# Norms that add pairs of squares on GpSimd before TensorE sums them over the features

## The reference

```python
def _normalize(x):
    xf = x.astype(jnp.float32)
    mu = jnp.mean(xf, axis=-1, keepdims=True)
    var = jnp.mean(jnp.square(xf - mu), axis=-1, keepdims=True)
    return (xf - mu) * lax.rsqrt(var + LN_EPS)
...
def rms_norm(x, g, eps=NORM_EPS):
    xf = x.astype(jnp.float32)
    y = xf * lax.rsqrt(jnp.mean(xf * xf, axis=-1, keepdims=True) + eps)
    return (y * g.astype(jnp.float32)).astype(x.dtype)
```

## Time and profile before

| | before |
|---|---|
| median of 3 runs | 4008.68 us (4008.21 to 4012.08) |
| the profiled execution | 4003.51 us, its span 4001.8 us |
| TensorE busy | 3569.2 us, 89% of the span, 27600 records |
| VectorE busy | 2124.3 us, 53% |
| ScalarE busy | 1295.8 us, 32% |
| GpSimd busy | 148.9 us, 4% |
| mean granted clock of TensorE | 0.905 |

### The profile page before, as it was taken

One profiled execution on the slowest core, in us unless ns is written; L12 is line 12 of the kernel. 1 busy time (PEld: TensorE's weight loads), 2 busy tenths in 40 slices (PEclk: granted clock), 3 DMA queues, 4 the chain that ended last, 5 costly groups with the idle time before them and its releaser, 6 DMA issues. The chain is left out here.

```text
span 4001.8 us, 64978 instructions
## 1 busy us (share of the span) xinstructions
PE 3569.2 (89%) x27600; PEld 3286.5 (82%) x27600; DVE 2124.3 (53%) x3151; ACT 1295.8 (32%) x1795; POOL 148.9 (4%) x148
## 2 busy tenths in 40 slices
PE   7679999999995889999997599999699999769799
PEld 5469999989973868999885489998499998458599
DVE  4527885557714425767345437673657543253254
ACT  1314444444412113444212134442434442211143
POOL 0001111100000100000000000000000000011000
PEclk9769999989997879999996699999799999878699
DMA  8407885447721005767531047674057443200142
GB/s 360 181 32 273 309 310 206 186 172 270 276 102 42 3 1 198 303 231 304 204 122 59 5 174 300 236 301 175 3 219 303 169 178 131 84 1 2 63 173 91
DMA packets 74190, 675.50 MB, mean 169 GB/s; under 512 B 8416, under 2 KB 12544, under 8 KB 52096
## 3 DMA queue, kind: packets, MB, share of 16 engines
q1 hardware_dynamic: 29824, 500.52, 32.2%
q10 hardware_dynamic: 41472, 151.01, 9.9%
q0 software_dynamic: 2688, 20.97, 1.6%
HBM read 668.25 MB, written 4.23 MB: 168 GB/s over the span
## 5 line engine op out<-in xcount | busy, mean ns | idle before, releaser
L1020 DVE TENSOR_TENSOR w_split<-ring,w_split 128x1024 fp32r<-128x1024 f32 x705 | 874.7, 1243 | 611.2 <-ACT w_split L915 608.9
L842 PE MATMUL banks<-u_split,w_split 128*128 128x256 f32 x3840 | 1092.8, 285 | 7.8 <-DVE w_split L1020 6.2
L915 ACT ACTIVATE w_split<-ring 128x1024 fp32r<-128x1024 f32 x705 | 742.9, 1057 | 1077.4 <-PE banks L844 861.0
L843 PE MATMUL banks<-u_split,w_split 128*128 128x256 f32 x3840 | 1090.6, 284 | 0.0
L844 PE MATMUL banks<-u_split,w_split 128*128 128x256 f32 x3840 | 1090.3, 284 | 0.0
L842 PEld LDWEIGHTS banks<-u_split,w_split 128*128 128x128 f32 x3840 | 742.1, 193 | 11.3 <-DVE w_split L1020 8.2
L427 PE MATMUL banks<-bufs,ring 128*128 128x256 f32 (+2 forms) x2880 | 659.7, 392 | 101.5 <-PEq L2710 24.0
L843 PEld LDWEIGHTS banks<-u_split,w_split 128*128 128x128 f32 x3840 | 741.7, 193 | 0.9
L844 PEld LDWEIGHTS banks<-u_split,w_split 128*128 128x128 f32 x3840 | 741.3, 193 | 0.0
L427 PEld LDWEIGHTS banks<-bufs,ring 128*128 128x128 f32 (+2 forms) x2880 | 553.3, 193 | 208.9 <-issue 85.5
L842 PE MATMUL banks<-h_split,w_split 128*128 128x256 f32 x1920 | 543.6, 283 | 2.9 <-DVE w_split L1020 2.9
(11 more groups left out here) (354 smaller groups left out, 3050.6 us busy)
## 6 DMA issues: line engine op xcount, KB each, us to landing
ring<-stream SPq DMA_DIRECT2D x147, 3072.0 KB, 10.9
bufs<-ada ACTq DMA_DIRECT2D x288, 512.0 KB, 11.1
bufs<-ada POOLq DMA_DIRECT2D x8, 2048.0 KB, 13.2
bufs<-ada SPq DMA_DIRECT2D x4, 2048.0 KB, 10.5
bufs<-c_rows SPq DMA_DIRECT2D x8, 512.0 KB, 4.3
bufs<-gate_rows POOLq DMA_DIRECT2D x32, 128.0 KB, 7.9
ring<-stream SPq DMA_DIRECT2D x4, 1024.0 KB, 5.1
ring<-stream SPq DMA_DIRECT2D x1, 2816.0 KB, 9.9
```

The lines of the kernel that those rows point to most:

```text
L842: pe.matmul(out, w(0), x(0), start=start, stop=False, skip_group_check=True)
L843: pe.matmul(out, w(0), x(1), start=False, stop=False, skip_group_check=True)
L915: nc.scalar.activation(w_split[:, slot, 0, :], piece(j, b), ACT.Copy).then_inc(high.sem, 1)
L1020: e = nc.vector.tensor_tensor(w_split[:, slot, 1, :], piece(j, b), w_split[:, slot, 0, :].bitcast(F32), ALU.subtract)
```

## The change

A new helper `pair_sums` runs on GpSimd. For each pair of chunks it waits for both squares and adds the odd chunk's to the even chunk's, in place, and counts an event (`x_paired`, or `center_paired` in the centering). `token_sums` is then called on the even chunks alone (`squares[:, 0:KC:2, :]`, n = 4) and waits for the paired event, so a norm takes 8 products. This is done in `center_stage` and in `NextNorm` of kind "root". Three kinds of stage get a GpSimd body for it. The FFN of the mixture of experts keeps the one it has, its next norm being of kind "mean". `first_ada_stage` and `pair_norm_stage` stay as they are.

```diff
--- before.py
+++ after.py
@@ -561,6 +561,14 @@
 MEAN_BANK, ROOT_BANK = 2, 3
 
 
+def pair_sums(core, pool, squares, squared, paired, per=1, offset=0):
+
+    for q in range(KC // 2):
+        pool.wait_ge(squared.sem, squared.at((2 * q + 2) // per + offset))
+        pool.tensor_tensor(squares[:, 2 * q, :], squares[:, 2 * q, :], squares[:, 2 * q + 1, :], ALU.add)\
+            .then_inc(paired.sem, paired.count(1))
+
+
 def token_sums(core, pe, rows, bank, arrived, summed, n=KC, per=1, first=0):
 
 
@@ -615,6 +623,11 @@
     def __init__(self, core, kind, squares, bank, eps=NORM_EPS, turn=0):
         self.core, self.kind, self.squares, self.bank, self.eps, self.turn = core, kind, squares, bank, eps, turn
         self.ready, self.squared, self.summed, self.spread = (core.event(n) for n in ("x_ready", "x_squared", "x_summed", "x_spread"))
+        self.paired = core.event("x_paired")
+
+    def on_gpsimd(self, pool):
+        if self.kind == "root":
+            pair_sums(self.core, pool, self.squares, self.squared, self.paired)
 
     def on_tensor(self, pe):
         core = self.core
@@ -625,7 +638,7 @@
             spread_tokens(core, pe, 0, MEAN_BANK, self.spread)
         else:
             inverse = core.event("inverse")
-            token_sums(core, pe, self.squares, self.bank, self.squared, self.summed)
+            token_sums(core, pe, self.squares[:, 0:KC:2, :], self.bank, self.paired, self.summed, n=KC // 2)
             pe.wait_ge(inverse.sem, inverse.at(self.turn + 1))
             spread_tokens(core, pe, 2, ROOT_BANK, self.spread)
 
@@ -684,11 +697,12 @@
         centered, squared, summed, spread, shifted = (
             core.event(n) for n in ("centered", "squared", "square_sum", "spread", "x_ready"))
         after = NextNorm(core, then, squares, 6, turn=1) if then else None
+        center_paired = core.event("center_paired")
 
         @block.tensor
         def _(pe):
             inverse = core.event("inverse")
-            token_sums(core, pe, squares, 4, squared, summed, per=2)
+            token_sums(core, pe, squares[:, 0:KC:2, :], 4, center_paired, summed, n=KC // 2)
             pe.wait_ge(inverse.sem, inverse.at(1))
             spread_tokens(core, pe, 2, ROOT_BANK, spread)
             if after:
@@ -705,6 +719,12 @@
             if then == "root":
                 after.square(act, KC - 1)
                 root_of_tokens(core, act, turn=1)
+
+        @block.gpsimd
+        def _(pool):
+            pair_sums(core, pool, squares, squared, center_paired, per=2)
+            if after:
+                after.on_gpsimd(pool)
 
         @block.vector
         def _(dve):
@@ -1011,6 +1031,11 @@
                     gate_loaded[q].made += 8 * n
                 gated.made += n
 
+        if gates is None and after:
+            @block.gpsimd
+            def _(pool):
+                after.on_gpsimd(pool)
+
         @block.vector
         def _(dve):
             ready = act_done if gates is None else gated
```

## The result

| | before | after |
|---|---|---|
| median, 5 runs each | 4011.2 us (4008.21 to 4012.1) | 3987.76 us (3984.6 to 3996.33) |
| ratio of the runs | | 0.9946, 95% interval 0.9932 to 0.9961 |
| the profiled execution | 4003.51 us, span 4001.8 | 3987.76 us, span 3986.1 |
| mean granted clock | 0.905 | 0.909 |

By the ratio of the runs the change is 21.7 us faster (15.6 to 27.3), 0.54%. Forecast were 17.3 us and 3991.4 us, in a range from 3982 to 4001. The forecast took its gain off the first three runs' 4008.7 us; all five have 4011.2.

The account below looks back on a forecast made before the run. It took TensorE's work and the waits for token sums (L597, 67.0 us) as the bound. Centerings 8.4, root norm 0.75, FFN ends 3.0 and projection ends 5.1 made 17.3 us off 4008.7: 3991.4 us, range 3982 to 4001.

Parts of the forecast that it names:

- What bounds the kernel: At fifteen norms nothing else runs beside the chain through the sums and L597, so what L597 gains, the span gains.
- Cost of one addition, 0.61 us: One GpSimd addition of 128x256 at the changed norms: 0.61 us, half of 1.267 less rounding; other end 0.91.
- The tail behind the last addition, 0.8 us fast and 1.1 slow: The last pair's four records, from TensorE's release to L597: 0.8 us at the faster pace, 1.1 at the slower.
- Centering, 2.8 us each: Three centerings: TensorE stays the later engine, sums take 3.5 us, L597 comes 2.8 us earlier each, 8.4 in all.
- FFN ends, 3.0 us: Seven FFN ends: L597 3.3 us after the sums' old start, 3.6 where records are slow; 3.0 us gained together.
- 0.91 there, 0.3 more: Three FFN ends before another FFN: the last addition, beside VectorE's L1111, takes 0.91 us, 0.3 more than elsewhere.
- Projection ends, 5.1 us: Four projection ends: TensorE waits only for the last pair; 1.0 us gained at three, 2.1 at the slow one.
- Signs of being wrong: Last addition over 0.1 us behind the last square, 1 us additions, late GpSimd barrier steps, or longer low clock stretches.
- The additions as the tail: Rival, chance 0.08: additions take 1.03 us and pile up at FFN ends; only 4 us gained in all.
- The clock: Rival, chance 0.10: emptier TensorE stays at the low clock behind norms; 18.7 us lost if at all eleven ends.
- The barrier: Rival, chance 0.05: GpSimd leaves the changed stages late; slower by 0.2% if leaving takes 4.4 us.
- 5 us each way: The widening of the forecast's range for TensorE clock steps of both signs at the changed norms.

Follow-up runs that it names:

- e3_no_add: The changed kernel without GpSimd's additions, TensorE summing only the even chunks' squares (another output): 3978.59 us, ratio 0.9927 to the kernel before.
- e4_low_late: The changed kernel with VectorE's piece of the next FFN's weights split behind the reciprocal at three FFN ends: 3986.11 us, ratio 0.9946 to the kernel before.
- e5_last_twice: The changed kernel with the last pair's addition made twice on GpSimd, first into a spare tile: 4001.4 us, ratio 0.9989 to the kernel before.

## Why the prediction was right, point by point

**What bounds the kernel.** That L597's wait is a chain of its own held in direction: both halves of the change shortened the time. It did not hold one for one. Where L605 came early enough, the table load set the root (`e3_no_add`), and where VectorE's piece came late, it set the barrier (`e4_low_late`).

**Cost of one addition, 0.61 us.** Too low: 0.72 to 0.74 us alone, even with VectorE idle. The forecast halved L2265's 1.267 us, but 256 more columns cost an estimated 0.54 us (1.267 less 0.725, if L2265's multiplication costs what an addition does), so that some 0.18 us would not shrink with the size. L1792, which has 255 columns and seemed to confirm 0.61, is a subtraction whose operands are shifted by a column; why it is shorter is open. It is not that it raises no semaphore: the spare addition of `e5_last_twice` raises none and takes 0.72.

**The tail behind the last addition, 0.8 us fast and 1.1 slow.** 0.70 (1085.13 to 1085.83) and 1.10. At the fast clock the two errors cancel: 0.09 + 0.61 + 0.8 was forecast from the last square to L605 and 1.50 measured. That this sum is exact is luck. At the slow clock it was 1.90 for 1.80.

**Centering, 2.8 us each.** 2.6: the addition is 0.1 us longer, and the sums take 3.58 us for 3.5. The term's reasoning, TensorE still the later one, held, with less slack than forecast.

**FFN ends, 3.0 us.** 2.0. The four plain ones gave 2.2 for 2.0, because at one of them the records turned fast. The step that failed is "0.91 there, 0.3 more" for the addition beside L1111: it took 1.60 us, and the three places lost 0.2 us in sum instead of gaining 1.0. The sentence on the Trainium skill beside it (SBUF — State Buffer, "SBUF: two separate sides": an exclusive lock, held for a whole instruction) gave the better price, and the trace agrees with it: L1136 starts at 1734.87 inside the addition of 1734.69 to 1735.42 and lasts 0.41 us longer than alone, then the last addition, which starts at 1735.48, ends 0.58 us behind L1136's end at 1736.50. I had priced it by scaling with the mean of L999, 1.88 us, of which one took 1.29 and the others 1.66 to 2.26; a wait behind another instruction does not scale with one's own size. The lock has a second half that I did not count: VectorE's own piece was held up by the addition before.

**Projection ends, 5.1 us.** 4.7; the gap of 0.6 us ahead of the last pair was there as forecast. What is missing is the first of the four, where the records were slow after the change and not before: 0.6 us for 1.0.

**Signs of being wrong.** One came true by its letter: in the centerings the last addition starts 0.35 us behind the last square, not within 0.1. TensorE covers it there; at the twelve root norms it is 0.08. An addition took over 1 us at three places, beside L1136.

**Rivals.** The additions as the tail: they are, at the twelve root norms, but at 0.73 us and not at 1.03. The clock: it did not turn against the change. TensorE stood at the lower level for 764 and 774 us in two traces of the kernel before, for 731 and 751 us in two of the changed one, and from 6 us ahead of L597 or L605 to 40 us behind it, over the eleven FFN and projection ends, for 88 and 99 us before and 71 and 65 after. The barrier: nothing of it is seen; TensorE is idle for 0.32 us at the stage changes of the earlier trace rows as before.

**The number.** 17.3 us forecast; 21.7 measured, then 15.2. In the first pair of traces the parts missed by -0.6, -0.1, +0.2, -1.2 and -0.4 us, so that 15.2 us stand at L605, and by other pairs of traces it is up to 18.1. The main part of the gain is thus accounted for by the chains. How much of the rest goes with the clock, or with the change through the clock, no run settled. The forecast's range adds 5 us for the clock below and only 2 above, against its own "5 us each way"; neither result needed that end.

## What to carry to other kernels

Look at which engine is late where two of them feed a sum: taking work from TensorE helped by 2.6 us where it was the late one (the centerings), and by 0.4 to 0.7 us where the last arrival was (the plain FFN ends), and there the price of the new step counts in full. Do not price a small instruction on GpSimd by halving a longer one: 0.61 us was forecast and 0.72 measured. Look for a VectorE instruction with two SBUF operands beside it: here each of the two held the other. Before moving such an instruction behind the norm, look at what it then ends: here it set the barrier. An idle engine can be the better place for a slower instruction, when the fast engine has its own work in front of it.

## What the runs showed of the hardware

An addition of 128x256 in float32 took 0.72 us on GpSimd and 0.42 on VectorE, with its two operands in SBUF. Beside a 128x1024 subtraction on VectorE it took 1.60 us and the subtraction 1.63 instead of 1.22. One kernel without a change had timed runs 18 us apart (0.45%), as its granted clock differed, and single stages came in a few fixed lengths over the twelve traces: 186.1 or 188.3 to 188.8 us for one, 32.4, 35.1 to 35.2 or 36.2 to 36.4 us for the next. ScalarE's table load ahead of the root took 1.28 us, and in `e3_no_add` the root started 0.01 us behind its end.
